# Value tiles of both mixers computed channel by channel and turned on TensorE

## The chip, the cores and the metric

The kernel runs on one core of one Trainium2 chip. The metric is the device time of one execution in microseconds. Four engines matter here: TensorE (PE in the profile) multiplies matrices and transposes, VectorE (DVE) and ScalarE (ACT) work elementwise, GpSimd (POOL) takes some splits of weights and some DMA issues; the SP queue issues the loads of weights.

## The reference, cut to what matters

Four layers over 512 tokens of width 1024: two of a first kind, then two of a second. Each has a mixer and one (first kind) or two (second kind) feed-forward blocks. A mixer begins with one projection `h @ w_in` whose columns are split among its heads:

```python
# first kind
(a_q, a_k, a_v, a_z, a_b, a_a, b_q, b_k, b_v, b_qi, b_ki, b_wi,
 c_q, c_f, c_i, c_g) = jnp.split(h @ w_in[l], SPLIT_POINTS, axis=-1)
vc = to_chunks(i.astype(f32), HG_HEADS, HG_DHEAD)      # c_i: 256 columns
# second kind
sb_q, sb_k, sb_v, fx_q, fx_k, fx_v                      # 256 columns each
```

`c_i` is the value of the gated recurrence HGRN2, `sb_v` and `fx_v` are the values of two attentions. All of them are needed with tokens on the partitions, because the products with them sum over tokens. Everything is float32.

## The kernel before, in words

Activations lie transposed: channels on the 128 partitions, the 512 tokens along the row. A float32 product is made of three: activation and weight are each split into a rounded high part and a low rest (`hh`, `hl`; `wh`, `wl`), and `product` (L1255) issues high by high, high by low and low by high, on L1257, L1258 and L1259.

A **tile** of the projection is 128 columns of `w_in`. `tile` (L1286) keeps a 128x128 block of weights in the array and moves all 512 tokens past it: 8 blocks of the contraction by 3 products, 24 matmuls of 512 columns, into one of PSUM banks 0 to 3. The result has channels on the partitions. `token_tile` (L1295) holds a block of 128 tokens in the array instead and moves the 128 weight columns past it: 4 token blocks by 8 by 3, 96 matmuls of 128 columns. Its result has tokens on the partitions. It is used for the value tiles: the last 2 of the 30 tiles of a first mixer (L1579), the last 4 of the 20 tiles of a second mixer (L1874). Over two layers of each kind that is 4 and 8 tiles, 12 in all.

Each engine runs its own instruction list in order; semaphores join them. For a tile n, SP loads the weights, ACT rounds them to `wh` (`split`, L759) once tile n-2 is done, DVE subtracts to get `wl` (L1991; in a first mixer POOL does the last ten, L691), PE multiplies (`mm_done` counts), and DVE or ACT takes the result out of its bank (`mm_free` counts).

**Around the value tiles of a first mixer.** ACT keeps the last ordinary tile (L960), splits the last weights and then computes gates: four small functions and a square root of the norms of queries and keys (L977 to L983), each behind a load of a function table, and a last table load for the softmax (L841). DVE has been picking the indexer's top keys (`pick`, L2327 to L2330); it waits for `silu_done` 13, which ACT gives after the last ordinary tile, then copies value tile 1 to `hgi` (L2364), makes the last picks, copies value tile 2, and gives `small_copied`. PE waits for that (L1584) and starts the sparse attention: `logits` (L1371), `turned` (L1381), `weighted` (L1393), 16 items in a pipeline over PE, DVE (`top`, `scale`, L2100 to L2107) and ACT (`exp` L841, `copy` L850). Beside it DVE takes the reciprocal of the norms (L2015, at item 0), and PE spreads them over the partitions (L1597, bank 4, every other item); it waits for the reciprocal at item 1.

**Around the value tiles of a second mixer.** DVE's list for tiles 16 to 20 holds splits two tiles ahead, four `fx_norm` of two instructions each (L2734), the copy of tile 16 to `gT` and then four copies of value tiles to `vtok` (L2769). ACT's holds the splits, four square roots, four GELUs on `gT` (L1137) and a table load (L1139). PE then waits until all four banks are free (L1883) and computes `scores(0)` (L1889), the first logits of the stick-breaking attention; ACT makes a softplus of them in three passes (L1145, L1149, L1154), DVE follows (L2790, L2795) with steps of the linear recurrence between (L2709 to L2720), and `scores(1)` waits for the fourth L2790.

Of the kernel before, what the change touches and what calls it, by code (L numbers as in the profile page):

```python
# [12 lines left out]
P = 128  # L13
# [135 lines left out]
def program(nc, a, out):  # L149
    ctx = ExitStack()  # L150
    with ctx:
# [3 lines left out]
        def ev(name):  # L155
            return Event(nc, ctx, name)
# [62 lines left out]
        def take(*shape):  # L219
# [6 lines left out]
            if len(shape) == 1:  # L226
# [153 lines left out]
        y_ready = ev("y_ready")  # L380
        x_ready = ev("x_ready")
        small_done = ev("small_done")
        small_copied = ev("small_copied")
        conv_done = ev("conv_done")
        conv_tap = ev("conv_tap")
        silu_done = ev("silu_done")
# [86 lines left out]
        small2_copied = ev("small2_copied")  # L473
        small_loaded = ev("small_loaded")

        in_mixers = [bc_done, bc_used, ix_go, s_raw, s_turn, small_hi, small_lo, small_done, small_copied,
                     conv_done, conv_tap, silu_done, ix_done, ix_relu, ix_used, lg_done, lg_max, at_exp,
                     at_norm, at_turn, at_copied, at_pv, at_out, g_in, g_abs, g_soft, g_cum, g_turn, g_cols,
                     g_ecol, dn_q, dn_p, dn_v, dn_exp, dn_r, rc_ws, rc_u, rc_o, rc_ds, rc_s, rc_oc, hg_ke,
# [250 lines left out]
        def _(s):  # L730
# [15 lines left out]
            def split(i=None, whole=False, first=None, after_out=False):  # L746
# [14 lines left out]
                place[1] += 1 if half or whole else 0  # L761
                place[2] = 0 if half or whole else 1

            def parts(shift=None):

                for k in range(KD):
                    h_sum.next(s)
                    if shift is None:
                        s.activation(hh[:, k, :], sq[:, k % 4, :], ACT.Copy).then_inc(h_hi.sem, 1)
                    else:  # L770
                        s.activation(hh[:, k, :], sq[:, k % 4, :], ACT.Identity, bias=shift(k))\
                            .then_inc(h_hi.sem, 1)
# [146 lines left out]
            for l in range(DEPTH):  # L919
# [43 lines left out]
                for j in range(22):  # L963
# [8 lines left out]
                    if 8 <= j < 16:  # L972
                        square(dnT[:, j - 8, :])
                s.drain().then_inc(silu_done.sem, 1)

                g_in.next(s)
                link(s.activation(head[:, 3:4], head[:, 0:1], ACT.Exp))  # L977
# [5 lines left out]
                s.activation(std[0:32, 0:P], ps[0:32, 7, 0:P], ACT.Sqrt, bias=epsc[0:32, 0:1])\  # L983
                    .then_inc(std_done.sem, 1)
                n_norm[0] += 1

                softmax(lg, pr, mx, sm, pT)

# [88 lines left out]
            for l in range(DEPTH):  # L1077
# [37 lines left out]

                for n in range(3, 21):
                    split()
                    if n == 4:
                        ff_in.next(s)
                        link(s.activation(ftmp[0:4, :], fF[0:4, :], ACT.Abs))  # L1120
                        link(s.activation(ftmp[0:4, :], ftmp[0:4, :], ACT.Exp, scale=-1.0))
                        s.activation(ftmp[0:4, :], ftmp[0:4, :], ACT.Ln, bias=1.0).then_inc(ff_ln.sem, 1)
                    if 8 <= n < 12:
                        gate(n - 8)
                    if 11 <= n < 15:
                        fx_raw.next(s)
                        square(fxraw[:, n - 11, :])
                    if n == 16:
                        row_root(7, P, 32, 64)
                    if n == 17:  # L1130
                        for j in range(4):
                            lr_rec.next(s)
                            s.activation(lr_t[j], lr_t[j], ACT.Sqrt).then_inc(lr_root.sem, 1)
                    if n == 18:
                        for j in range(4):
                            conv_done.next(s)
                            s.activation(gT[:, j, :], gT[:, j, :], ACT.Gelu_apprx_tanh).then_inc(g_gelu.sem, 1)  # L1137

                s.preload_act_table_set("natural_log_exp_and_others")  # L1139

# [25 lines left out]
                for h in range(4):  # L1166
                    if h < 3:
                        soft(h + 1)
                    for b in range(NT):
                        sb_min.next(s)  # L1170
                        w_ = wsb[:, b, 0:T - b * P]
                        s.activation(w_, w_, ACT.Exp).then_inc(sb_exp.sem, 1)
                lr_y.next(s)
                for j in range(4):
                    square(uT[:, j, :])

# [42 lines left out]
        def _(pe):  # L1219
# [72 lines left out]
                                k == 0, k == KD - 1)  # L1292
                m.then_inc(mm_done.sem, 1)

            def token_tile(N, pool=False):  # L1295

                w, b = parts_ready(pool), bank()
                for n in range(NT):
                    for k in range(KD):
                        m = product(ps[:, b, N * n:N * n + N], hh[:, k, n * P:(n + 1) * P], wh[:, w, k, 0:N],  # L1300
                                    hl[:, k, n * P:(n + 1) * P], wl[:, w, k, 0:N], k == 0, k == KD - 1)
                m.then_inc(mm_done.sem, 1)

            def out_pair(src):

# [233 lines left out]
            for l in range(DEPTH):  # L1539
# [36 lines left out]
                            pe.wait_ge(ix_relu.sem, 12)  # L1576
                        stair_part(n - 9, 8)
                n_norm[0] += 1
                token_tile(P, True)  # L1579
                token_tile(P, True)  # L1580
                place[1] += 16


                small_copied.next(pe)  # L1584
                pe.wait_ge(ix_relu.sem, 12)

                def beside(i):

                    m = i // 2
                    if i % 2 and m < 8:  # L1590
                        if m == 0:
                            pe.wait_ge(rec_done.sem, n_norm[0])
                        else:
                            pe.wait_ge(bc_used.sem, m)
                        for t in range(NT):
                            j = NT * m + t
                            x = pe.matmul(ps[:, BESIDE, t * P:(t + 1) * P], ident[:, j:j + 1].broadcast_to([P, P]),  # L1597
                                          rstd[:, 0:P], start=True, stop=True)
                        x.then_inc(bc_done.sem, 1)
                    if i == 17:  # L1600
                        g_cum.next(pe)
                        pe.wait_ge(bc_used.sem, 8)
                        for n in range(NT):
                            for o, src in enumerate((gg, bet)):
                                at_ = 8 * n + 4 * o
                                x = pe.matmul(ps[:, BESIDE, at_:at_ + 4], src[0:4, n * P:(n + 1) * P],
                                              ident[0:4, 0:4], start=True, stop=True)
                        x.then_inc(g_turn.sem, 1)
# [205 lines left out]
            for l in range(DEPTH):  # L1814
# [41 lines left out]
                for n in range(2, 17):  # L1856
# [12 lines left out]
                    if n == 15:  # L1869
                        small2_copied.next(pe)  # L1870
                        pe.wait_ge(lr_sig.sem, 4)
                        for m in range(4):
                            column_cast(m)
                for n in range(4):  # L1874
                    token_tile(P)
                place[1] += 10

                def scores(h):
# [39 lines left out]
                              start=b == 0, stop=b == NT - 1).then_inc(sb_pv.sem, 1)  # L1918

                scores(0)  # L1920
                for m in range(NT * 4 + 2):
                    if m % NT == 0 and m // NT < 3:
                        scores(m // NT + 1)
                    if m < NT * 4:
                        past(m)
                    if m >= 2:
                        breaks(m - 2)
                pe.wait_ge(nr_used.sem, 4)
                row_sums(4, 4)

                def beside(i):
# [30 lines left out]
        def _(v):  # L1962
# [302 lines left out]
            for l in range(DEPTH):  # L2265
# [93 lines left out]
                mm_done.seen[id(v)][1] += 10  # L2359
                n_mm[0] += 10  # L2360
                v.wait_ge(silu_done.sem, 13)
                for j in range(2):
                    b = filled()
                    v.tensor_copy(hgi[:, :, j * P:(j + 1) * P], ps[:, b, :].rearrange("p (n c) -> p n c", n=NT))  # L2364
                    free()
                    if j:
                        v.sem_inc(small_copied.sem, 1)
                    pick(4)

                def beside(i):  # L2370

# [2 lines left out]
                    if i == 1:  # L2374
                        g_soft.next(v)
                        link(v.tensor_scalar(head[:, 3:4], head[:, 3:4], -1.0, None, ALU.mult))
                        link(v.scalar_tensor_tensor(gg[0:4, :], gg[0:4, :], 0.0, gtmp[0:4, :], ALU.max, ALU.add))
                    if i == 3:
                        link(v.tensor_scalar(gg[0:4, :], gg[0:4, :], head[:, 3:4], None, ALU.mult))
                    if i == 5:  # L2380
                        v.tensor_tensor_scan(gg[0:4, :], reset[0:4, :], gg[0:4, :], 0.0, ALU.mult, ALU.add)\
# [245 lines left out]
            for l in range(DEPTH):  # L2627
# [110 lines left out]
                for n in range(1, 21):  # L2738
# [11 lines left out]
                    if n == 17:  # L2750
                        fx_norm(2)
                        fx_norm(3)
                        v.drain()
                    b = filled()
                    if n <= 2:
                        v.tensor_scalar(sbq[:, n - 1, :], ps[:, b, :], 0.125, None, ALU.mult)
                    elif n <= 4:
                        v.tensor_copy(sbk[0:64, 2 * (n - 3), :], ps[0:64, b, :])
                        v.tensor_copy(sbk[64:128, 2 * (n - 3) + 1, :], ps[64:128, b, :])
                    elif n <= 8:  # L2760
                        j = n - 5
                        taps(uT[:, j, :], b, lambda s_: par[:, 1, B2_CW + 4 * s_ + j:B2_CW + 4 * s_ + j + 1], 4,
                             par[:, 1, B2_CB + j:B2_CB + j + 1])
                    elif n <= 12:
                        v.tensor_copy(fxraw[:, n - 9, :], ps[:, b, :])
                    elif n <= 16:
                        v.tensor_copy(gT[:, n - 13, :], ps[:, b, :])
                    else:
                        v.tensor_copy(vtok[:, :, (n - 17) * P:(n - 16) * P],  # L2769
                                      ps[:, b, :].rearrange("p (n c) -> p n c", n=NT))  # L2770
                    free()
                    if n == 4:
                        ff_ln.next(v)
# [42 lines left out]
                for b in range(5):  # L2816
                    if b < 4:
                        raw(0, b)
                    if b:
                        masked(0, b - 1)  # L2820
                    lr_step(1)
                v.wait_ge(small_loaded.sem, l * 208 + 208)
                for h in range(4):
# [100 lines left out]
```

## Time and profile before

| | |
|---|---|
| Median of three executions | 4055.58 us |
| Lowest and highest | 4048.1 and 4056.75 us |
| The profiled execution's own time | 4050.49 us |
| Its span in the trace | 4048.7 us |
| Mean granted clock of TensorE | 0.97 |
| PE busy | 3819.4 us, 94% |
| DVE busy | 2191.7 us, 54% |
| ACT busy | 1163.6 us, 29% |

The span is what the trace covers; 1.8 us lie around it. Busy shares are averages over stages. In rows of the timeline the first number is the start in us from the span's beginning, the second the length in us, then engine, line, operation, output and input, and in brackets the engine's idle time before it and what ended that.

### The profile page before, as it was taken

Reading aid. Unit: us, or ns where it says so; the run is one execution under the profiler, and the core shown is the slowest. Engines: PE = TensorE matmul, PEld = TensorE weight load, DVE = VectorE, ACT = ScalarE, POOL = GpSimd, SP = SyncE. Lnnn points to the kernel's source line nnn. Section 1 sums busy time; section 2 is a strip of 40 time slices with the busy share of each in tenths; the row PEclk is TensorE's granted clock in tenths of the full one; section 3 lists DMA queues with packets and bytes.
Section 4 is the critical chain, followed back from the end, with each engine's and each line's share of the span. In section 5 each row is a group of like instructions: output and inputs, shape, how many; then the busy total and the mean of one; then the engine's idle time right before and its main releaser. Section 6 shows DMA issues by size and latency. Waiting matters only on the chain.

```text
span 4048.7 us, 50706 instructions
## 1 busy us (share of the span) xinstructions
PE 3819.4 (94%) x18550; PEld 3027.4 (75%) x18550; DVE 2191.7 (54%) x3552; ACT 1163.6 (29%) x1715; POOL 302.2 (7%) x503
## 2 busy tenths in 40 slices
PE   7998889998998889998999998899999999999999
PEld 5778648886777648887888785588878887756887
DVE  4767548854767548855554456355343336444432
ACT  2331323322431323322222234222222223332221
POOL 1110001100020001110110100011000001000000
PEclk9998899999999899999999999999999999999999
DMA  3310025542220025542554320255433332103332
GB/s 87 84 36 1 1 74 161 163 122 78 73 56 1 1 58 162 163 136 82 165 163 122 95 63 1 76 165 164 121 93 94 88 101 74 42 21 83 93 94 94
DMA packets 580037, 359.75 MB, mean 89 GB/s; under 512 B 20398, under 2 KB 559776, under 8 KB 579872
## 3 DMA queue, kind: packets, MB, share of 16 engines
q1 hardware_dynamic: 554464, 281.43, 25.0%
q0 software_dynamic: 25408, 76.11, 6.3%
q8 instruction: 105, 1.72, 0.2%
q14 instruction: 60, 0.49, 0.0%
HBM read 355.35 MB, written 2.10 MB: 88 GB/s over the span
## 4 chain that ended last, share of the span: by engine, by line
PE 87%; DVE 8%; ACT 2%; issue 2%; DVEq 1%; SPq 0%; POOL 0%; DMA 0%; ACTq 0%; POOLq 0%
PE ps L1257 17%; PE ps L1258 17%; PE ps L1259 17%; PE ps L1497 6%; PE ps L1501 6%; PE ps L1500 6%; PE ps L1310 5%; PE ps L1628 3%; PE ps L1413 1%; PE ps L1393 1%; PE ps L1371 1%; PE ps L1790 1%; DVE wl L1991 1%; PE ps L1460 1%; PE ps L1346 1%
## 5 line engine op out<-in xcount | busy, mean ns | idle before, releaser
L1257 PE MATMUL ps<-hh,wh 128*128 128x512 f32 x2816 | 1119.1, 397 | 42.4 <-DVE hl L2050 17.2
L1258 PE MATMUL ps<-hl,wh 128*128 128x512 f32 x2816 | 1103.9, 392 | 0.0
L1259 PE MATMUL ps<-hh,wl 128*128 128x512 f32 x2816 | 1103.7, 392 | 0.0
L1991 DVE TENSOR_TENSOR wl<-wring,wh 128x1024 fp32r<-128x1024 f32 x476 | 581.2, 1222 | 788.9 <-ACT wh L759 782.0
L759 ACT ACTIVATE wh<-wring 128x1024 fp32r<-128x1024 f32 x496 | 522.9, 1056 | 992.5 <-PE ps L1497 506.2
L1257 PEld LDWEIGHTS ps<-hh,wh 128*128 128x128 f32 x2816 | 533.5, 189 | 176.7 <-issue 44.3
L1259 PEld LDWEIGHTS ps<-hh,wl 128*128 128x128 f32 x2816 | 533.0, 189 | 113.0
L1258 PEld LDWEIGHTS ps<-hl,wh 128*128 128x128 f32 x2816 | 534.0, 190 | 108.6 <-issue 1.9
L1497 PE MATMUL ps<-ah,wh 128*128 128x512 f32 x1056 | 411.9, 390 | 2.0 <-DVE wl L1991 2.0
L1501 PE MATMUL ps<-ah,wl 128*128 128x512 f32 x1056 | 410.9, 389 | 0.0
L1500 PE MATMUL ps<-al,wh 128*128 128x512 f32 x1056 | 410.8, 389 | 0.0
L684 POOL DMA_DIRECT2D wada<-in_w_ada x384 | 206.4, 538 | 2059.0 <-DVE ada_sum L2135 1293.7
L1497 PEld LDWEIGHTS ps<-ah,wh 128*128 128x128 f32 x1056 | 198.2, 188 | 43.6 <-DVE wl L1991 2.8
L1501 PEld LDWEIGHTS ps<-ah,wl 128*128 128x128 f32 x1056 | 198.2, 188 | 41.2
L1500 PEld LDWEIGHTS ps<-al,wh 128*128 128x128 f32 x1056 | 198.2, 188 | 40.8
L2139 DVE SCALAR_TENSOR_TENSOR ada_sum<-wada,cact,ada_sum 128x384 f32<-128x384 f32 x288 | 177.8, 617 | 76.1 <-DMA wada<-in_w_ada 34.6
L1310 PE MATMUL ps<-arena,wring 128*128 128x512 f32 x448 | 197.1, 598 | 6.2 <-issue 3.1
L1310 PEld LDWEIGHTS ps<-arena,wring 128*128 128x128 f32 x448 | 84.5, 191 | 117.4 <-issue 114.0
L878 ACT ACTIVATE sq<-ps 128x512 f32<-128x512 f32 x88 | 52.7, 599 | 405.9 <-PE ps L1259 374.7
L1628 PEld LDWEIGHTS ps<-arena 128*128 128x128 f32 x1152 | 135.6, 197 | 20.0 <-ACT arena L994 7.6
L1628 PE MATMUL ps<-arena 128*128 128x128 f32 x1152 | 137.6, 281 | 10.9 <-ACT arena L994 5.4
L2193 DVE TENSOR_TENSOR sq<-sq,ps 128x512 f32<-128x512 f32 x88 | 60.5, 687 | 147.7 <-PE ps L1259 147.7
(396 smaller groups left out, 4041.3 us busy)
## 6 DMA issues: line engine op xcount, KB each, us to landing
wring<-in_w_ffn_up SPq DMA_DIRECT2D x176, 512.0 KB, 4.9
wada<-in_w_ada POOLq DMA_DIRECT2D x384, 192.0 KB, 2.7
wring<-in_w_in SPq DMA_DIRECT2D x98, 512.0 KB, 5.1
wring<-in_ffn_w_up SPq DMA_DIRECT2D x88, 512.0 KB, 5.0
wring<-in_w_ffn_down SPq DMA_DIRECT2D x64, 512.0 KB, 3.6
wring<-in_w_out SPq DMA_DIRECT2D x32, 512.0 KB, 4.9
wring<-in_ffn_w_down SPq DMA_DIRECT2D x32, 512.0 KB, 3.6
wring<-in_w_ffn_down SPq DMA_DIRECT2D x16, 384.0 KB, 3.2
```

Of the source, the lines that this page charges most:

```text
L684: g.dma_start(wada[:, i % 2, :], src[:, m, bass.ds(col + at_, ADA_W)])\
L759: s.activation(wh[:, n_split[0] % 2, :, :], wring[:, p, half, :, :], ACT.Copy).then_inc(w_hi.sem, 1)
L1257: pe.matmul(dst, w, h, start=first, stop=False)
L1258: pe.matmul(dst, w, hlo, start=False, stop=False)
L1259: return pe.matmul(dst, wlo, h, start=False, stop=last)
L1310: m = pe.matmul(ps[:, b, :], wring[:, p, half, k, :], src[:, k, :], start=k == 0, stop=k == KD - 1)
L1497: first = pe.matmul(ps[:, b, :], wh[:, w, j, :], ah[:, at_], start=k == 0, stop=False)
L1500: pe.matmul(ps[:, b, :], wh[:, w, j, :], al[:, at_], start=False, stop=False)
L1501: m = pe.matmul(ps[:, b, :], wl[:, w, j, :], ah[:, at_], start=False, stop=k == NF - 1)
L1628: m = pe.matmul(ps[:, b, n * P:(n + 1) * P], lhsT(n), rhs(n), start=True, stop=True)
L1991: v.tensor_tensor(wl[:, w, :, :], wring[:, p, h, :, :], wh[:, w, :, :].bitcast(F32), ALU.subtract)\
L2139: i = v.scalar_tensor_tensor((ada_out if k == KD - 1 else ada_sum)[:, :], wada[:, k % 2, :], cact[:, k:k + 1], ada_sum[:, :], ALU.mult, AL ...
```

## The change

The 12 value tiles are computed by `tile`, with channels on the partitions. ACT copies each result from its bank to an SBUF buffer and frees the bank (`raw`); PE turns the buffer by four 128x128 transposes into another bank (`turn_raw`); DVE copies that bank to `hgi` or `vtok`, with the shape it had before (`turned`). Three semaphores, `v_raw`, `v_turn` and `v_copied`, take the place of `small_copied`. In a first mixer the buffers are `cbuf`, the turned banks are 4 and 2, and the second tile is turned inside the attention. In a second mixer the buffers are `sq`, the bank is 4, and the fourth tile is turned behind `scores(0)`.

```diff
 # ACT
+            def raw(dst, b, tiles_behind):
+                at_ = mm_done.seen[id(s)]
+                s.wait_ge(mm_done.sem, at_[0] + at_[1] - tiles_behind)
+                s.activation(dst, ps[:, b, :], ACT.Copy).then_inc(v_raw.sem, 1)
+                s.drain().then_inc(mm_free.sem, 1)
...
                 s.drain().then_inc(silu_done.sem, 1)
+                raw(cbuf[:, 0, :], 2, 1)
                 g_in.next(s)
...
                     .then_inc(std_done.sem, 1)
                 n_norm[0] += 1
+                raw(cbuf[:, 1, :], 3, 0)
                 softmax(lg, pr, mx, sm, pT)
...
                 for n in range(3, 21):
                     split()
+                    if n >= 19:
+                        raw(sq[:, n - 19, :], n - 19, 2)
...
+                for j in (2, 3):
+                    raw(sq[:, j, :], j, 3 - j)
                 s.preload_act_table_set("natural_log_exp_and_others")
...
                 lr_y.next(s)
+                s.wait_ge(v_copied.sem, 4)
 # PE
-            def token_tile(N, pool=False):
...
+            def turn_raw(b, src):
+                v_raw.next(pe)
                 for n in range(NT):
+                    m = pe.transpose(ps[:, b, n * P:(n + 1) * P], src[:, n * P:(n + 1) * P], ident[:])
+                m.then_inc(v_turn.sem, 1)
...
-                token_tile(P, True)
-                token_tile(P, True)
+                tile(True)
+                tile(True)
                 place[1] += 16
-                small_copied.next(pe)
-                pe.wait_ge(ix_relu.sem, 12)
+                turn_raw(BESIDE, cbuf[:, 0, :])
+                pe.wait_ge(mm_free.sem, mm_free.seen[id(pe)][0] + mm_free.seen[id(pe)][1] + 2)
...
                     if i % 2 and m < 8:
                         if m == 0:
+                            pe.wait_ge(v_copied.sem, 1)
                             pe.wait_ge(rec_done.sem, n_norm[0])
...
+                    if i == 2:
+                        turn_raw(2, cbuf[:, 1, :])
+                    if i == 4:
+                        pe.wait_ge(v_copied.sem, 2)
...
-                for n in range(4):
-                    token_tile(P)
+                for j in range(4):
+                    tile()
+                    if j == 1:
+                        pe.wait_ge(nr_used.sem, 1)
+                    if j > 1:
+                        pe.wait_ge(v_copied.sem, j - 1)
+                    if j:
+                        turn_raw(4, sq[:, j - 1, :])
...
                 scores(0)
+                pe.wait_ge(v_copied.sem, 3)
+                turn_raw(4, sq[:, 3, :])
 # DVE
                 v.wait_ge(silu_done.sem, 13)
-                for j in range(2):
-                    b = filled()
-                    v.tensor_copy(hgi[:, :, j * P:(j + 1) * P], ps[:, b, :].rearrange("p (n c) -> p n c", n=NT))
-                    free()
-                    if j:
-                        v.sem_inc(small_copied.sem, 1)
-                    pick(4)
+                def turned(b, dst):
+                    v_turn.next(v)
+                    v.tensor_copy(dst, ps[:, b, :].rearrange("p (n c) -> p n c", n=NT)).then_inc(v_copied.sem, 1)
+                pick(4)
+                pick(4)
+                turned(BESIDE, hgi[:, :, 0:P])
...
                     if i == 3:
+                        turned(2, hgi[:, :, P:2 * P])
...
+                    if n > 16:
+                        mm_done.seen[id(v)][1] += 1
+                        n_mm[0] += 1
+                        if n > 17:
+                            turned(4, vtok[:, :, (n - 18) * P:(n - 17) * P])
+                        continue
...
                     if b:
                         masked(0, b - 1)
+                    if b == 2:
+                        turned(4, vtok[:, :, 3 * P:4 * P])
                     lr_step(1)
```

## Rows read from the trace of the kernel before

**Rows 1.** The page, parts 1 and 4: busy time of PE, and the chain by engine

```profile
PE 3819.4 (94%) x18550; PEld 3027.4 (75%) x18550; DVE 2191.7 (54%) x3552; ACT 1163.6 (29%) x1715; POOL 302.2 (7%) x503
...
PE 87%; DVE 8%; ACT 2%; issue 2%; DVEq 1%; SPq 0%; POOL 0%; DMA 0%; ACTq 0%; POOLq 0%
```

**Rows 2.** Timeline of ACT around the value tiles, first mixer of layer 0

```profile
217.00 0.60 ACT L960 ACTIVATE arena<-ps 128x512 f32<-128x512 f32 x1 [3.95 <-PE ps L1259]
...
222.38 0.60 ACT L960 ACTIVATE arena<-ps 128x512 f32<-128x512 f32 x1 [3.84 <-PE ps L1259]
...
224.02 1.28 ACT L977 ACT_TABLE_LOAD   x1
...
232.04 0.36 ACT L983 ACTIVATE std<-ps,epsc 32x128 f32<-32x128 f32 x1
232.42 1.28 ACT L841 ACT_TABLE_LOAD   x1
245.58 0.40 ACT L841 ACTIVATE arena<-arena 128x128 f32<-128x128 f32 x1 [11.88 <-DVE arena L2100]
```

**Rows 3.** Timeline of DVE, the same stretch

```profile
233.15 0.69 DVE L2364 COPY arena<-ps 128x512 f32<-128x512 f32 x1 [14.81 <-PE ps L1259]
233.96 0.69 DVE L2327 MAX8 arena<-arena 128x8 f32<-128x512 f32 x1
...
238.52 0.43 DVE L2330 TENSOR_SCALAR arena<-arena 128x512 f32<-128x512 f32 x1
243.84 0.69 DVE L2364 COPY arena<-ps 128x512 f32<-128x512 f32 x1 [4.90 <-PE ps L1259]
...
245.47 0.94 DVE L2015 RECIPROCAL rstd<-std 32x128 f32<-32x128 f32 x1
...
254.44 0.42 DVE L2100 CUSTOM_DVE_ANT_0 arena<-ps,arena 128x256 f32<-128x256 f32 x1 [3.05 <-issue]
```

**Rows 4.** Timeline of PE, head of that attention

```profile
246.46 2.07 PE L1597 MATMUL ps<-rstd,ident 128*128 128x128 f32 x8 [1.02 <-DVE rstd L2015]
...
248.75 0.42 PE L1381 MATMUL ps<-ident,arena 128*128 128x128 f32 x1
248.96 0.63 PE L1371 MATMUL ps<-arena 128*128 128x128 f32 x2
249.86 0.47 PE L1381 MATMUL ps<-ident,arena 128*128 128x128 f32 x1 [0.26 <-DVE arena L2107]
```

**Rows 5.** Timeline of PE, eight transposes at full clock, earlier in layer 0

```profile
77.35 1.03 PE L1551 MATMUL ps<-ident,arena 128*128 128x128 f32 x8
```

**Rows 6.** Stretches: us, then PE, PEld, DVE, ACT, POOL busy (count), clock, DMA

```profile
233.00:244.00 11.00, 10.73 (x97) 10.59 (x95) 5.62 (x12) 0.70 (x1) 0.00 (x0) 1.00 0.00 0
244.00:262.00 18.00, 15.53 (x61) 11.52 (x62) 11.50 (x42) 4.97 (x20) 0.00 (x0) 0.62 0.00 1
262.00:300.00 38.00, 37.21 (x232) 27.05 (x231) 25.23 (x79) 13.70 (x35) 0.00 (x0) 1.00 0.01 1
```

**Rows 7.** Timeline of ACT around the value tiles, second mixer of its layer 0

```profile
2388.12 1.06 ACT L759 ACTIVATE wh<-wring 128x1024 fp32r<-128x1024 f32 x1 [4.69 <-PE ps L1259]
...
2398.85 1.06 ACT L759 ACTIVATE wh<-wring 128x1024 fp32r<-128x1024 f32 x1 [3.71 <-PE ps L1259]
...
2432.89 1.14 ACT L1145 ACTIVATE arena<-ps 128x512 f32<-128x512 f32 x2 [21.02 <-PE ps L1889]
```

**Rows 8.** Timeline of DVE, the same stretch

```profile
2393.65 0.69 DVE L2767 COPY arena<-ps 128x512 f32<-128x512 f32 x1
...
2401.08 3.04 DVE L2734 SCALAR_TENSOR_TENSOR arena<-arena,lb,ps 64x512 f32<-64x512 f32 x4
...
2420.23 0.69 DVE L2769 COPY arena<-ps 128x512 f32<-128x512 f32 x1 [7.58 <-PE ps L1259]
2430.95 0.69 DVE L2769 COPY arena<-ps 128x512 f32<-128x512 f32 x1 [10.03 <-PE ps L1259]
2435.77 0.69 DVE L2790 SCALAR_TENSOR_TENSOR hT<-ps,arena 128x512 f32<-128x512 f32 x1 [4.13 <-ACT arena L1154]
...
2439.36 0.29 DVE L2790 SCALAR_TENSOR_TENSOR hT<-ps,arena 128x128 f32<-128x128 f32 x1
```

**Rows 9.** Timeline of PE, the first two score groups of that mixer

```profile
2431.72 2.42 PE L1889 MATMUL ps<-arena 128*128 128x512 f32 x8 [0.81 <-DVEq L2090]
2439.70 4.37 PE L1889 MATMUL ps<-arena 128*128 128x512 f32 x8 [5.56 <-DVE hT L2790]
```

More of the change, by code:

```diff
@@ L382, in program @@
         small_done = ev("small_done")
-        small_copied = ev("small_copied")
+        v_raw = ev("v_raw")
+        v_turn = ev("v_turn")
+        v_copied = ev("v_copied")
         conv_done = ev("conv_done")
@@ L474, in program @@
         small_loaded = ev("small_loaded")
-        in_mixers = [bc_done, bc_used, ix_go, s_raw, s_turn, small_hi, small_lo, small_done, small_copied,
+        in_mixers = [bc_done, bc_used, ix_go, s_raw, s_turn, small_hi, small_lo, small_done, v_raw, v_turn, v_copied,
                      conv_done, conv_tap, silu_done, ix_done, ix_relu, ix_used, lg_done, lg_max, at_exp,
@@ L1293, in tile @@
                 m.then_inc(mm_done.sem, 1)
-            def token_tile(N, pool=False):
-                w, b = parts_ready(pool), bank()
+            def turn_raw(b, src):
+                v_raw.next(pe)
                 for n in range(NT):
[L1299 to L1302, printed above, removed]
+                    m = pe.transpose(ps[:, b, n * P:(n + 1) * P], src[:, n * P:(n + 1) * P], ident[:])
+                m.then_inc(v_turn.sem, 1)
             def out_pair(src):
@@ L1928, in _ @@
                 pe.wait_ge(nr_used.sem, 4)
+                pe.wait_ge(v_copied.sem, 4)
                 row_sums(4, 4)
@@ L2358, in _ @@
                 half[0] = 1 - half[0]
-                mm_done.seen[id(v)][1] += 10
-                n_mm[0] += 10
+                mm_done.seen[id(v)][1] += 12
+                n_mm[0] += 12
                 v.wait_ge(silu_done.sem, 13)
-                for j in range(2):
-                    b = filled()
-                    v.tensor_copy(hgi[:, :, j * P:(j + 1) * P], ps[:, b, :].rearrange("p (n c) -> p n c", n=NT))
-                    free()
-                    if j:
-                        v.sem_inc(small_copied.sem, 1)
-                    pick(4)
+                def turned(b, dst):
[4 more added lines that the diff above has]
+                turned(BESIDE, hgi[:, :, 0:P])
                 def beside(i):
@@ L2765, in _ @@
                         v.tensor_copy(fxraw[:, n - 9, :], ps[:, b, :])
-                    elif n <= 16:
+                    else:
                         v.tensor_copy(gT[:, n - 13, :], ps[:, b, :])
-                    else:
-                        v.tensor_copy(vtok[:, :, (n - 17) * P:(n - 16) * P],
-                                      ps[:, b, :].rearrange("p (n c) -> p n c", n=NT))
                     free()
```

## The prediction

> **What bounds the kernel now.** I read the page first: PE is busy 94% of the span and makes up 87% of the chain of work that ended last [rows 1]. Work taken from PE counts unless something else is ready to end the same stretch, so the question for each of the 12 value tiles is which engine is late next. For that I read the timelines of ACT, DVE and PE around the value tiles, first mixer [rows 2 to 4] and second mixer [rows 7 to 9], and then the granted clock [rows 6]. In both places the reader should see the same thing: ACT and DVE sit waiting for PE's last matmul of a tile (11.88 us before ACT's first exponential, 10.03 us before DVE's last copy, 21.02 us before ACT's softplus) [rows 2, 8, 7], while PE has no gap: 97 matmuls fill 10.73 of 11 us at full clock [rows 6]. PE sets the end of the value stretch in all four mixers.
>
> **The price of a tile.** An ordinary tile: ACT takes two of them out at 217.00 and 222.38, both times straight after PE, 5.4 us apart [rows 2]; that is 24 matmuls, 0.224 us each. A value tile: DVE's copies at 233.15 and 243.84 are 10.7 us apart [rows 3], those at 2420.23 and 2430.95 the same [rows 8]; 96 matmuls, 0.111 us each. So a value tile made as an ordinary one takes 5.3 us less of PE, 63.6 us over 12. The rest of the working is what does not reach the end.
>
> What stands against this is a rule for the spacing alone. A matmul of 128 columns costs here half of one of 512, not a quarter. The Trainium skill ("TensorE: Matmul & The Clock Gate", back-to-back issue gap) gives for an isolated bf16 matmul at the high clock columns / 2.4 + 2.5 ns; by that both forms would take about 5.3 us, and the change would gain 2 us before its costs. The same section says that streams with a weight load for each matmul go slower than this at 128 columns. The trace disagrees with the formula and agrees with the caveat: both forms were timed here in the place where they are used, and I go by the rows.
>
> **First mixer, two tiles, one layer.** PE ends tile 2 not at about 243.7 but 2 x 5.3 = 10.6 us earlier, at 233.1. Then step by step:
> - POOL's split takes about as long as for the ordinary tiles before, which ran without a gap, so its weights are in time: 0.
> - ACT now waits for value tile 1 in front of its gate work. The tile ends at 222.3 + 5.4 = 227.7; the copy takes 0.60 as at 222.38 [rows 2], a drain 0.1, so the gate work begins at 228.5 in place of 224.02: 4.5 us later. The root of the norms, at 232.04 before, ends at 232.40 + 4.5 = 236.9 [rows 2]. Queued behind the wait are all the gate functions, that root and the table load for the softmax.
> - DVE has the picks (4.99 us, from 233.96 to 238.95 [rows 3]) to do between 224 and 229, hidden under the two tiles. The first turned copy is hidden too (0.69, at about 233.8).
> - The attention's head needs the reciprocal of the norms, because PE spreads it at item 1 before it goes on [rows 4]. Before, that reciprocal began at 245.47 [rows 3], held back by DVE's second copy. Now it can begin at 236.95, held back by ACT. **Gain 8.5 us, not 10.6**: what is late next is ACT's gate work.
> - The second raw copy (0.6) and the table load (1.28) stand between root and first exponential, which comes at 238.8, 1.9 us behind the start of the reciprocal in place of 0.1. PE turned the first item 3.3 us behind that start (248.75 [rows 4] less 245.47 [rows 3]) and needs the exponential plus about 1.0 us of DVE, 2.9 us: it just fits, 0 to 0.3 lost.
> - PE turns value tile 2 at item 2, at half clock (the clock averaged 0.62 from 244 to 262 [rows 6]). Two logit matmuls and a transpose start 0.21 us apart there (248.75 to 248.96 [rows 4]), so four transposes cost 0.85; at full clock eight end 1.03 us after the first begins, some 0.45 for four [rows 5]. PE waited 0.26 for DVE just behind [rows 4]. I take 0.85, between 0.2 and 1.1.
> - DVE's second turned copy (0.69) falls at item 3, ahead of 3.05 us in which DVE did nothing [rows 3]: 0. PE's wait for it at item 4 comes later than that: 0.
>
> Net 8.5 - 0.9 = 7.6 us; for two layers **15.2 us**.
>
> **Second mixer, four tiles, one layer.** PE begins value tile 1 at 2388.0, where ACT's split was waiting for the tile before [rows 7]. The order of the splits has to keep up with 5.4 us a tile:
> - ACT splits tile 18's weights at 2388.12, has its GELUs until about 2395.1 (the last waits for DVE's copy at 2393.65 [rows 8]), and splits tile 19's at 2395.1 where it waited until 2398.85 before [rows 7]. DVE follows at 2396.2 and is done at 2397.4; PE wants the weights at 2398.9. Margin 1.5 us.
> - DVE's norm step, 3.04 us [rows 8], then runs to 2400.5, its split for tile 20 to 2401.8; PE wants that at about 2404.8. Margin 3 us. All raw and turned copies (0.6 and 0.69) fit in the idle time of both engines.
> - PE turns tiles 1 and 2 between products, 0.45 us each at full clock [rows 5], 0.9 in all. Tile 3's turn lies beside ACT's copy of tile 4, which frees the last bank as DVE's copy of 0.69 did before [rows 8]: 0. ACT loads its table behind that copy now (1.28, as in rows 2) while PE starts the scores, 1.2 us ahead of the first softplus pass (2431.72 [rows 9] to 2432.89 [rows 7]): 0 to 0.3.
> - DVE's fourth turned copy falls among the four L2790, which run back to back with the recurrence from 2435.77 to 2439.36 [rows 8]; PE's second scores wait for the last of them [rows 9]. 0.6 to 0.7 on the path.
>
> Net 4 x 5.3 - 0.9 - 0.65 - 0.15 = 19.5 us; for two layers **39.0 us**.
>
> Sum: 15.2 + 39.0 = 54.2 us off the profiled execution's own 4050.5 us, 3996.3. Its median of three is 4055.6, 5 us above, and the lowest 4048.1; I allow 2 us for that and forecast **3998 us**, 1.4% less. A measurement of this kernel tells about 0.2%, 8 us, from no change.
>
> **What is not in the rows.** How PE's clock behaves when it idles at a new moment. Before, it fell at the head of the first attention: a mean of 0.62 over 18 us with PE busy 15.5 us [rows 6], so some 13.7 us at half clock. Had all been at full clock, up to 6 us less; another such stretch, up to 6 us more. PE will idle again at this head, now from 233.6 to 238 and wholly, so I take the same low stretch, and 3 us either way for the pair of layers.
>
> **Rivals.**
> - **A: PE's whole gain arrives.** The gate work on ACT is short enough, or the attention does not wait for the reciprocal: 10.6 - 0.9 in a first mixer, in all 58 us, 3992 to 3994. For: ACT was idle 11.88 us [rows 2]. Against: of these, 4.5 + 1.9 are used up and the reciprocal is needed at item 1 [rows 4]. 12%.
> - **B: the handovers cost more.** Each of 12 turns waits for ACT and DVE across semaphores, or the split order stalls tile 3 of a second mixer (margin 1.5 us): 1 us more per tile, 12 us, 4010. For: ACT is now in front of PE in each tile. Against: the margins above. 12%.
> - **C: slower, by the clock.** After its wait at the attention's head PE stays at half clock. From 262 to 300 PE is busy 37.2 of 38 us at clock 1.00 [rows 6]; at half of it that would take up to 37 us longer. It decides from 54 / 4, some 14 us per mixer, which is 14 us of full-clock work done at half clock; all of that stretch low in four mixers gives +94 us, 4145. For: a wholly idle PE of 4 us is new. Against: the clock came back after 13.7 us in the trace under just such mixed work [rows 6]. 2%.
> - **D: a tile costs the same in either form**, so nothing is gained and 12 turns and waits remain: 12 x 0.3 to 0.8, 4054 to 4060. This is the formula of the skill quoted above; against it stand two timings in rows 2, 3 and 8. 2%.
>
> The forecast itself has 72%, with a range of its own of 3990 to 4006. A and B carry the range to **3986 to 4010**. Faster by over 0.2%: forecast, A, B, 96%; within: 2%; slower: 2%.
>
> **What would show it.** Right: 512-column groups on L1257 to L1259 with 12 x 24 matmuls more and no 128-column ones left; the new ACT copies following PE's last matmul; in the first mixer PE idle about 4 us ahead of L1597 with the reciprocal behind ACT's root, the root 4.5 us behind its old distance from the last kept tile; the second mixer's first scores 43.7 - 20.2 = 23.5 us behind the split that was at 2388.12. Wrong: matmuls of a value tile more than 0.23 us apart, an idle PE between value tiles of a second mixer, a clock of 0.5 beyond the first 20 us of an attention, or first scores later than 25 us.

## The result, and the profile after

The change made the kernel faster: ratio 0.9854 of the times before, 95% interval 0.9827 to 0.988. The median of four executions is 3994.3 us (3986.5 to 4005.0) against 4056.2 us (4048.1 to 4057.1). The forecast was 3998 us in a range of 3986 to 4010. The profiled execution took 4004.99 us by itself, its span 4003.3 us: it is the slowest of the four, and only 45.5 us shorter than the profiled one before, where 54.2 were forecast. The medians differ by 61.9 us. Where the other 9 of the profiled execution went is a question for the experiments.

The page of the changed kernel, part 1 (PE), part 4 (the chain by engine) and part 5 (one of the three product lines):

```profile
PE 3773.6 (94%) x17734; PEld 2970.2 (74%) x17734; DVE 2190.5 (55%) x3552; ACT 1169.6 (29%) x1727; POOL 302.3 (8%) x503
...
PE 86%; DVE 8%; ACT 3%; issue 2%; DVEq 1%; SPq 0%; ACTq 0%; POOL 0%; DMA 0%; POOLq 0%
...
L1273 PE MATMUL ps<-hh,wh 128*128 128x512 f32 x2912 | 1158.0, 398 | 42.2 <-DVE hl L2078 16.9
```

L1273 to L1275 are L1257 to L1259 of before. Each has 2912 matmuls of 512 columns in place of 2816: 96 more, 3 x 96 = 12 tiles x 24. PE has 816 instructions less: 12 x (96 - 24) = 864 less for the products, 48 more for the transposes. The chain is what it was but for a percent that passed from PE to ACT [rows 1].

**First mixer of layer 0.** Timeline of ACT, answering to [rows 2]:

```profile
222.55 0.60 ACT L969 ACTIVATE arena<-ps 128x512 f32<-128x512 f32 x1 [3.83 <-PE ps L1275]
...
227.99 0.60 ACT L770 ACTIVATE arena<-ps 128x512 f32<-128x512 f32 x1 [3.89 <-PE ps L1275]
228.69 1.28 ACT L987 ACT_TABLE_LOAD   x1
...
236.71 0.36 ACT L993 ACTIVATE std<-ps,epsc 32x128 f32<-32x128 f32 x1
236.97 0.57 ACT L770 ACTIVATE arena<-ps 128x512 f32<-128x512 f32 x1
237.64 1.28 ACT L850 ACT_TABLE_LOAD   x1
238.93 0.40 ACT L850 ACTIVATE arena<-arena 128x128 f32<-128x128 f32 x1
```

Timeline of DVE, the same stretch, answering to [rows 3]:

```profile
233.94 0.69 DVE L2393 COPY arena<-ps 128x512 f32<-128x512 f32 x1 [4.72 <-PE ps L1315]
...
237.10 0.94 DVE L2043 RECIPROCAL rstd<-std 32x128 f32<-32x128 f32 x1 [2.26 <-ACT std L993]
...
242.56 0.68 DVE L2393 COPY arena<-ps 128x512 f32<-128x512 f32 x1
...
244.43 0.42 DVE L2128 CUSTOM_DVE_ANT_0 arena<-ps,arena 128x256 f32<-128x256 f32 x1 [0.81 <-DVE arena L2409]
```

Timeline of PE, answering to [rows 4, 5] (L1315 are the new transposes):

```profile
233.23 0.60 PE L1315 MATMUL ps<-ident,arena 128*128 128x128 f32 x4
233.67 0.61 PE L1385 MATMUL ps<-arena 128*128 128x128 f32 x4
238.19 1.47 PE L1612 MATMUL ps<-rstd,ident 128*128 128x128 f32 x8 [3.91 <-DVE rstd L2043]
...
240.27 1.06 PE L1315 MATMUL ps<-ident,arena 128*128 128x128 f32 x4
241.13 0.63 PE L1385 MATMUL ps<-arena 128*128 128x128 f32 x2
```

Stretches of the changed kernel, columns as in [rows 6]:

```profile
222.00:233.20 11.20, 11.20 (x51) 9.23 (x50) 4.77 (x10) 6.56 (x9) 3.70 (x3) 1.00 0.44 129
...
238.20:256.00 17.80, 16.83 (x90) 12.07 (x91) 13.77 (x51) 8.02 (x29) 0.00 (x0) 0.90 0.01 1
```

What to see: the reciprocal that the attention's head needs now waits 2.26 us for ACT's root (it had waited for DVE's copies before), and PE idles 3.91 us ahead of L1612. Measured from the last kept tile, the reciprocal begins 14.55 us later (222.55 to 237.10), before 23.09 (222.38 to 245.47): 8.54 us won. The four transposes at full clock cost 0.44 us (233.23 to 233.67), those inside the attention at half clock 0.86 (240.27 to 241.13). One thing is not as forecast: the stretch at the attention's head had a mean clock of 0.90, not 0.62 [rows 6].

**Second mixer of its layer 0.** Timeline of ACT, answering to [rows 7]:

```profile
2381.72 1.06 ACT L761 ACTIVATE wh<-wring 128x1024 fp32r<-128x1024 f32 x1 [4.69 <-PE ps L1275]
...
2388.64 1.04 ACT L761 ACTIVATE wh<-wring 128x1024 fp32r<-128x1024 f32 x1
...
2392.60 1.06 ACT L761 ACTIVATE wh<-wring 128x1024 fp32r<-128x1024 f32 x1 [2.43 <-PE ps L1275]
...
2404.45 0.60 ACT L770 ACTIVATE sq<-ps 128x512 f32<-128x512 f32 x1 [5.32 <-PE ps L1275]
2405.14 1.28 ACT L1154 ACT_TABLE_LOAD   x1
2406.44 0.99 ACT L1160 ACTIVATE arena<-ps 128x512 f32<-128x512 f32 x2
```

Timelines of DVE and PE there, answering to [rows 8] and [rows 9]:

```profile
2404.89 0.69 DVE L2393 COPY arena<-ps 128x512 f32<-128x512 f32 x1 [5.22 <-PE ps L1315]
2409.18 0.69 DVE L2823 SCALAR_TENSOR_TENSOR hT<-ps,arena 128x512 f32<-128x512 f32 x1 [3.61 <-ACT arena L1169]
...
2412.32 0.68 DVE L2393 COPY arena<-ps 128x512 f32<-128x512 f32 x1
...
2413.37 0.29 DVE L2823 SCALAR_TENSOR_TENSOR hT<-ps,arena 128x128 f32<-128x128 f32 x1
```

```profile
2404.25 0.60 PE L1315 MATMUL ps<-ident,sq 128*128 128x128 f32 x4
2405.13 2.42 PE L1914 MATMUL ps<-arena 128*128 128x512 f32 x8 [0.28 <-ACTq L771]
```

From the split for tile 18 to the first scores it took 2405.13 - 2381.72 = 23.41 us. The prediction has 23.5 there, from 43.7; the rows give 43.6 (2388.12 to 2431.72), so its own figure should have been 23.4. To the first softplus pass it took 24.72 us (2406.44 - 2381.72) in place of 44.77, 20.05 less. DVE's turned copy at 2412.32 stands between the softplus steps: they take 4.19 us from first to fourth, before 3.59 (2435.77 to 2439.36).

### The profile page after: what moved, and what is told of

Read it like the earlier page. It is cut to its first block, busy times and chain, and to the rows that moved or that the text cites. A ratio compares the mean times of both kernels' runs of the same rounds, so it can differ in the third digit from the quotient of the medians.

```text
span 4003.3 us, 49102 instructions
## 1 busy us (share of the span) xinstructions
PE 3773.6 (94%) x17734; PEld 2970.2 (74%) x17734; DVE 2190.5 (55%) x3552; ACT 1169.6 (29%) x1727; POOL 302.3 (8%) x503
## 4 chain that ended last, share of the span: by engine, by line
PE 86%; DVE 8%; ACT 3%; issue 2%; DVEq 1%; SPq 0%; ACTq 0%; POOL 0%; DMA 0%; POOLq 0%
PE ps L1273 17%; PE ps L1274 16%; PE ps L1275 16%; PE ps L1511 6%; PE ps L1515 6%; PE ps L1514 6%; PE ps L1324 5%; PE ps L1647 3%; PE ps L1427 1%; PE ps L1407 1%; PE ps L1809 1%; PE ps L1385 1%; DVE wl L2019 1%; PE ps L1474 1%; PE ps L1360 1%
## 5 line engine op out<-in xcount | busy, mean ns | idle before, releaser
L1273 PE MATMUL ps<-hh,wh 128*128 128x512 f32 x2912 | 1158.0, 398 | 42.2 <-DVE hl L2078 16.9
L1274 PE MATMUL ps<-hl,wh 128*128 128x512 f32 x2912 | 1142.3, 392 | 0.0
L1275 PE MATMUL ps<-hh,wl 128*128 128x512 f32 x2912 | 1141.6, 392 | 0.0
L1273 PEld LDWEIGHTS ps<-hh,wh 128*128 128x128 f32 x2912 | 551.9, 190 | 179.9 <-issue 43.9
L1275 PEld LDWEIGHTS ps<-hh,wl 128*128 128x128 f32 x2912 | 551.8, 189 | 117.2
L1274 PEld LDWEIGHTS ps<-hl,wh 128*128 128x128 f32 x2912 | 552.6, 190 | 112.7 <-issue 1.9
L1511 PEld LDWEIGHTS ps<-ah,wh 128*128 128x128 f32 x1056 | 198.2, 188 | 43.6 <-DVE wl L2019 2.8
L1647 PE MATMUL ps<-arena 128*128 128x128 f32 x1152 | 138.4, 282 | 10.4 <-ACT arena L1005 4.9
```

The source lines that it names most:

```text
L1273: pe.matmul(dst, w, h, start=first, stop=False)
L1274: pe.matmul(dst, w, hlo, start=False, stop=False)
L1275: return pe.matmul(dst, wlo, h, start=False, stop=last)
L1511: first = pe.matmul(ps[:, b, :], wh[:, w, j, :], ah[:, at_], start=k == 0, stop=False)
L1647: m = pe.matmul(ps[:, b, n * P:(n + 1) * P], lhsT(n), rhs(n), start=True, stop=True)
```

## The experiments

Ratios are to the kernel before, which ran on the same chip beside each group.

**The changed kernel once more**, for a second profile.

> The changed kernel once more, for a second profile. Theory 1 (place by place): the value tiles and their heads give what they gave in the first profile in every execution (7 to 11 us in a first mixer by the attention, 20 us in a second mixer by the first softplus pass), and the 9.5 us that the first profile lost after that, from 7.9 us ahead at the start of layer 0's delta recurrence to 1.6 us behind at its end, are half-clock time that fell there in that execution; in a second profile that loss is absent or elsewhere. Rival 2 (the change slows the recurrence): it is there again, 8 us or more. Ratio by theory 1 0.984 to 0.988, 3990 to 4000 us.

Measured: ratio 0.9857 (0.9835 to 0.9879), median 3994.6 us. The heads gave what they gave. But layer 0's recurrence was slow again: its first output came 7.5 us ahead of before (386.98 against 394.45), its eighth 2.2 us behind (426.17 against 423.97). In the first profile it was 7.7 us ahead at the first output and 1.8 behind at the root of the norms that follows the eighth (430.58 against 428.81). ACT's outputs of the recurrence (one per chunk of 64 tokens) in the kernel before:

```profile
394.45 0.38 ACT L1029 ACTIVATE hT<-ps 128x256 f32<-128x256 f32 x1 [6.66 <-PE ps L1708]
400.51 0.38 ACT L1029 ACTIVATE hT<-ps 128x256 f32<-128x256 f32 x1 [5.68 <-PE ps L1708]
404.49 0.38 ACT L1029 ACTIVATE hT<-ps 128x256 f32<-128x256 f32 x1 [3.60 <-PE ps L1708]
```

and in the changed kernel's first profile:

```profile
386.71 0.38 ACT L1040 ACTIVATE hT<-ps 128x256 f32<-128x256 f32 x1 [6.66 <-PE ps L1727]
393.93 0.38 ACT L1040 ACTIVATE hT<-ps 128x256 f32<-128x256 f32 x1 [6.83 <-PE ps L1727]
401.14 0.38 ACT L1040 ACTIVATE hT<-ps 128x256 f32<-128x256 f32 x1 [6.83 <-PE ps L1727]
407.35 0.38 ACT L1040 ACTIVATE hT<-ps 128x256 f32<-128x256 f32 x1 [5.83 <-PE ps L1727]
411.33 0.38 ACT L1040 ACTIVATE hT<-ps 128x256 f32<-128x256 f32 x1 [3.60 <-PE ps L1727]
```

And two stretches of the changed kernel that lie in it (columns as in [rows 6]):

```profile
386.00:401.00 15.00, 15.00 (x68) 14.02 (x67) 4.10 (x12) 0.77 (x2) 0.00 (x0) 0.50 0.00 0
401.00:430.60 29.60, 27.59 (x185) 23.72 (x184) 13.31 (x34) 5.79 (x12) 0.00 (x0) 0.80 0.01 1
```

A chunk takes 7.21 us at half clock (the first stretch) and 3.98 at full clock; for that, a stretch of the kernel before:

```profile
404.60:429.00 24.40, 22.13 (x184) 19.92 (x182) 12.76 (x34) 5.86 (x12) 0.00 (x0) 1.00 0.01 2
```

Before, one step was slow (6.06 us), now three are (7.22, 7.21 and 6.21). PE is busy all the time in the slow stretch, so this is not a wait.

**One mixer kind alone.** The change in the second mixers, then in the first mixers, the other kind as before (`token_tile` and `small_copied` kept for it).

> The change in the second mixers alone, the first mixers as before. Prediction's sum: 19.5 us per layer, 39.0 us, ratio 0.990. If the handovers cost 1 us more per tile (rival B): 31 us, 0.992. In its profile the gap between the split for tile 18 and the first softplus pass should be 23.3 to 23.6 us in place of 44.8.

> The change in the first mixers alone. Prediction's sum: 7.6 us per layer, 15.2 us, ratio 0.996. If the changed kernel's first profile is the rule and the recurrence gives it back (rival 2): about 6 us in all, 0.9985. If the shorter half-clock stretch at the attention's head is a lasting part of the gain (11 us per layer): 22 us, 0.9945.

Measured: second alone 0.9905 (0.9888 to 0.9922), median 4010.8 us, 38.5 us less; first alone 0.9963 (0.9947 to 0.9979), median 4035.2 us, 15.0 us less than 4049.65. The sums of the prediction were 39.0 and 15.2. The figure of 23.3 to 23.6 us in the first of these expectations names the wrong end: it holds for the first scores, the softplus pass is 1.3 us behind (24.72 in the changed kernel, and 24.72 here: 2387.23 to 2411.95). Rival B (31 us) lies just outside the interval (0.9922 is 31.6 us), and so does a lasting gain of 22 us in the first mixers (0.9947 is 21.5 us); the 6 us of rival 2 lie outside it too (0.9979 is 8.5 us).

**The form of the tile alone**: only what PE multiplies is changed; the turn is left out.

```diff
-                token_tile(P, True)
-                token_tile(P, True)
+                tile(True)
+                tile(True)
...
-                    token_tile(P)
+                    tile()
```

> The 12 value tiles are made with channels on the partitions, and DVE copies them as before; the turn into token order, ACT's copy and the second bank are left out, so the values enter the attentions and the recurrence in the wrong order. This is the price of the tile's form alone: 5.3 us for each of 12 tiles; in a first mixer 0.8 us less of it arrives, because DVE's last picks (4.99 us) then end between the two copies at 233.7 in place of 233.2. Sum 62 us, ratio 0.9847. The changed kernel against it shows what the handover costs: by the prediction 8 us (54 against 62). If both forms cost the same (rival D): 1.000.

Measured: 0.9831 (0.9812 to 0.985), median 3984.0 us; that is 68 us (61 to 76), where 62 were expected. Rival D is out: the two forms do not cost the same. Against the changed kernel of the same group (3994.6) it is 10.7 us faster, where 8 were expected. Rows of it, ACT and then DVE (before's line numbers):

```profile
2365.96 1.06 ACT L759 ACTIVATE wh<-wring 128x1024 fp32r<-128x1024 f32 x1 [4.69 <-PE ps L1259]
...
2389.66 1.14 ACT L1145 ACTIVATE arena<-ps 128x512 f32<-128x512 f32 x2 [10.45 <-PE ps L1889]
```

```profile
234.21 0.94 DVE L2015 RECIPROCAL rstd<-std 32x128 f32<-32x128 f32 x1
```

Split to softplus takes 23.70 us here and 24.72 with the turns: 1.0 us for the handovers of a second mixer as far as this pass, where the prediction had 0.9 + 0.15. In a first mixer its last kept tile was at 221.22, so the reciprocal begins 12.99 us behind, against 14.55 with the turns.

**ACT's first raw copy moved behind the gate work**, and **with it DVE's fourth turned copy** moved behind the softplus steps (both moves).

```diff
                 s.drain().then_inc(silu_done.sem, 1)
-                raw(cbuf[:, 0, :], 2, 1)
...
                 n_norm[0] += 1
+                raw(cbuf[:, 0, :], 2, 1)
                 raw(cbuf[:, 1, :], 3, 0)
...
-                    if b == 2:
+                    if b == 4:
                         turned(4, vtok[:, :, 3 * P:4 * P])
```

> The changed kernel, with ACT's copy of a first mixer's value tile 1 moved behind the gate work and the root of the norms. The root then ends at 232.4 again in place of 236.9, both raw copies follow it, and what is late next is DVE's first turned copy (about 234.0 to 234.6): the reciprocal begins at 234.9 in place of 237.1. Theory 1 (ACT's gate work behind the new wait set the head): 2.2 us less at the reciprocal and 3 to 4 at the first exponential, per layer, 4 to 7 us in all, ratio 0.9843 to 0.985. Rival (the head is set by PE's turn and DVE): no change, 0.986. The clock's low stretches will again fall elsewhere, several us either way in one execution.

> The same, and in a second mixer DVE's turned copy of value tile 4 moved from among the four softplus steps (after the third) to after the fourth. By theory 1 it then lies in the 3.3 us in which DVE waits for the next softplus: 0.6 us less per layer for the second scores, 1.2 in all; ratio 0.984 to 0.985. If the copy was hidden anyway: as gates_first.

Measured: first move alone 0.9843 (0.9825 to 0.9862), median 3993.5 us; both 0.983 (0.9815 to 0.9846), median 3980.8 us. DVE of the first move alone (its last kept tile at 221.35):

```profile
232.75 0.69 DVE L2392 COPY arena<-ps 128x512 f32<-128x512 f32 x1 [4.72 <-PE ps L1314]
...
233.56 0.94 DVE L2042 RECIPROCAL rstd<-std 32x128 f32<-32x128 f32 x1
```

The reciprocal begins 12.21 us behind the kept tile, 2.34 less than in the changed kernel (14.55), and right behind DVE's turned copy. ACT's first exponential comes 12.88 us behind the kept tile (234.23), in the changed kernel 16.38 (238.93 - 222.55): 3.50 us less, where 3 to 4 were expected. So ACT's gate work behind the new wait was what held the head, and DVE is next, as expected. DVE of both moves, in a second mixer:

```profile
2384.15 0.69 DVE L2822 SCALAR_TENSOR_TENSOR hT<-ps,arena 128x512 f32<-128x512 f32 x1 [3.61 <-ACT arena L1168]
...
2387.74 0.29 DVE L2822 SCALAR_TENSOR_TENSOR hT<-ps,arena 128x128 f32<-128x128 f32 x1
...
2389.61 0.68 DVE L2392 COPY arena<-ps 128x512 f32<-128x512 f32 x1
```

First to fourth step take 3.59 us again: 0.60 won per layer as far as this step.

**Dead work ahead of layer 0's recurrence**, in the changed kernel:

```diff
                 dn_q.next(pe)
+                for _ in range(80 if l == 0 else 0):
+                    pe.transpose(ps[:, 0, 0:P], ident[:], ident[:])
```

> The changed kernel with 80 dead transposes (8.7 us at full clock) on PE ahead of layer 0's gated delta rule, so that this stage and the recurrence start where they started in the kernel before (delta recurrence's first output near 394.4 in place of 386.7). Theory 1b (the loss in layer 0's recurrence comes from when the stage starts relative to the clock's changes, not from the change's own work): the low stretch in the recurrence is 13.7 us again in place of 27.3 and 34.1, the recurrence takes 9 us less, and the dead work is paid back: the end of that recurrence comes within 2 us of where it was. Rival 2 (something in the change slows the recurrence): low stretch still 27 us or more, everything from there 8.7 us later, 4003 us median.

Measured: 0.9885 (0.987 to 0.99), median 4004.8 us, 7.8 to 10.5 us more than the changed kernel's medians (3994.3 to 3997.0), which ran in other groups. Rival 2 had 4003 us. In its profile the recurrence's first outputs are:

```profile
392.46 0.38 ACT L1040 ACTIVATE hT<-ps 128x256 f32<-128x256 f32 x1 [6.65 <-PE ps L1729]
399.68 0.38 ACT L1040 ACTIVATE hT<-ps 128x256 f32<-128x256 f32 x1 [6.83 <-PE ps L1729]
405.89 0.39 ACT L1040 ACTIVATE hT<-ps 128x256 f32<-128x256 f32 x1 [5.83 <-PE ps L1729]
409.88 0.38 ACT L1040 ACTIVATE hT<-ps 128x256 f32<-128x256 f32 x1 [3.60 <-PE ps L1729]
```

Two slow steps (7.22 and 6.21 us), neither one (theory 1b) nor three (rival 2). The recurrence began at 392.46, not near 394.4 as meant, and this execution was already 1.3 us ahead of the changed kernel's first profile at the last kept tile (221.26 against 222.55). Its eighth output came at 425.38, there 422.84, and the root behind it at 430.21, there 430.58. So of the 5.75 us between the first outputs a part was gained back by the end of the recurrence in this execution. Over its executions the dead work was not paid back. Each theory is half right: the length of the low stretch changes with the start of the stage, but no gain in time is shown. At equal clock (last table below) the dead work costs 4.1 us, less than its own 8.7, but four executions in a group without the changed kernel can't settle that.

From the first to the eighth output layer 0's recurrence took, in the profiles, what the third column says. The last two columns split each execution in two: at ACT's split for tile 18 in the first of the second mixers, behind both first mixers, and from there to the end of the span.

| kernel | first output at | first to eighth, us | split for tile 18 at | from there to the end, us |
|---|---|---|---|---|
| before | 394.45 | 29.5 | 2388.12 | 1660.6 |
| second mixers alone | 393.49 | 29.5 | 2387.23 | 1620.1 |
| changed, three profiles | 386.71, 386.98, 385.78 | 36.1, 39.2, 36.1 | 2381.72, 2378.39, 2370.25 | 1621.6, 1621.8, 1621.9 |
| first mixers alone | 386.44 | 36.1 | 2371.07 | 1660.2 |
| form alone | 379.10 | 29.5 | 2365.96 | 1619.2 |
| first move | 382.05 | 36.1 | 2369.82 | 1622.0 |
| both moves, two profiles | 376.57, 383.21 | 29.7, 36.1 | 2356.68, 2371.07 | 1619.9, 1619.7 |
| dead work | 392.46 | 32.9 | 2379.97 | 1621.9 |

The loss of 7 to 10 us is no fixed cost of the change: one profile of both moves, which does the same work, is without it, and so is the form alone, though both start the recurrence earlier still. It is no chance of single executions either: all three profiles of the changed kernel have it, and those of the first mixers alone and of the first move. What it goes by is not shown.

Behind the split, where only the second mixers are changed, the three profiles of the changed kernel gain 39.0, 38.8 and 38.7 us (39.0 forecast). Ahead of it, where only the first mixers are changed, they gain 6.4, 9.7 and 17.9 us (15.2 forecast), and the first mixers alone 17.0. So what the profiles differ by lies ahead of the split. There the rest of layer 0 decides, work that the change does not touch: from the recurrence's eighth output to the last kept tile of layer 1 it takes 727.3 us before (mean clock 0.96), 728.7 in the changed kernel's first profile (0.95), but 719.2 and 718.6 in the other two and 718.3 with the first mixers alone (0.97 each). All three profiles of the changed kernel lose in the recurrence; two get as much or nearly as much back behind it, the first does not, and that is about its missing 9 us.

**The changed kernel and both moves on one chip.**

> The changed kernel on one chip with the next, for their difference. Theory 1: ratio to the kernel before 0.984 to 0.987.

> The version with both moves again. By the heads of its stages (2 to 4 us less in a first mixer, 0.6 in a second) 5 to 9 us less than the changed kernel, ratio 0.982 to 0.985; if the first comparison's 11 us were chance, no difference.

Measured: 0.9851 (0.9821 to 0.9882) and 0.9842 (0.9814 to 0.987), medians 3997.0 and 3996.1 us. The raw times do not tell the two apart: 0.9 us, where the heads had promised 5 to 9. They scatter with the clock, which the results list for each execution: the twelve executions of first mixers alone reach from 4020.75 us at a mean clock of 0.974 to 4049.71 at 0.966. I fitted one slope to 93 executions (one level per kernel), which gives -3.4 us for each 0.001 of mean clock, and read each kernel at 0.970, with what is left as scatter (3.2 us; without the slope 7.7). One execution of the changed kernel is left out: it is listed with a mean clock of 0.926 and took 3993.6 us like its neighbours, where the slope would add some 150 us. With it in, the slope is -0.5 and the changed kernel's level 58.4 us below the one before, so the table rests on leaving it out:

| kernel | executions | at clock 0.970, us | less than before |
|---|---|---|---|
| before | 37 | 4051.8 +- 1.1 | |
| changed | 13 | 3997.2 +- 1.8 | 54.5 |
| second mixers alone | 6 | 4010.3 +- 2.6 | 41.5 |
| first mixers alone | 12 | 4036.7 +- 1.8 | 15.1 |
| form alone, no turn | 5 | 3990.9 +- 2.9 | 60.9 |
| first move | 5 | 3989.4 +- 2.8 | 62.3 |
| both moves | 11 | 3994.2 +- 2.0 | 57.6 |
| dead work | 4 | 4001.3 +- 3.2 | 50.5 |

The +- are 95% bounds of the fit; they leave out differences between chips. Both moves is 3.1 us faster than the change by this reading (0.4 to 5.6 by the fit); the heads of the stages say 5.9 (2 x 2.34 + 2 x 0.60). That the first move alone reads lower than both moves shows how far such a reading can be trusted: some 5 us.

## Why the prediction was right

- **The price of a tile** held: the value stretch of the first mixer is full (PE 11.20 of 11.20 us) and the tiles are 5.4 us apart; 12 tiles less their handovers gave 54.5 us at equal clock, 54.2 were forecast. By raw medians the three groups gave 61.9, 55.0 and 64.0 us. The formula of the Trainium skill ("TensorE: Matmul & The Clock Gate", back-to-back issue gap) for isolated matmuls, weighed against it in the prediction, would have given 2 us before costs; the runs disagree with it.
- **First mixer.** What was late next was named: ACT's gate work. The root ended 4.5 us later against the kept tile, the reciprocal began 8.54 us earlier (8.5 forecast), the first exponential 1.83 us behind it (1.9), the turn at half clock cost 0.86 us (0.85), DVE's second turned copy lay in idle time. The kernel with the change in the first mixers alone gave 15.0 us (15.2). Of the 10.6 us that PE saves in the mixer the prediction left 10.6 - 8.5 = 2.1 us behind; moving ACT's copy alone won 2.34 us, so that was this copy. How the parts add up is in some measure luck, though. In layer 1 the reciprocal came 8.63 us earlier against the kept tile, as in layer 0, but the recurrence's first output 10.4 us earlier in the changed kernel's first profile (1312.46 - 1151.54 = 160.92 in place of 1322.62 - 1151.31 = 171.31), 10.5 and 10.4 in the other two and 11.1 with the first mixers alone, where the prediction has 7.6. That and the clock's gains and losses in layer 0 lie on both sides of 15.2 and about cancel.
- **Second mixer.** First scores 23.41 us behind the split (23.4), the split order without a stall (tile 19's weights split at 2388.64, tile 20's at 2392.60 with 2.43 us of waiting ahead), table load level with the scores, DVE's copy 0.60 us on the path. Alone: 38.5 us (39.0), and 38.7 to 39.0 behind the split in the changed kernel's three profiles. The prediction's 43.7 us should have been 43.6, which makes 23.4 us; no step hangs on it.
- **Rival A** fell with the wait of 2.26 us for the root. Its total did not decide it: the measured median (3994.3) fits its 3992 to 3994 as well as the forecast. **Rival B** fell with 1.0 us of handovers in a second mixer as far as the softplus, not 4. **Rival C**, slower by the clock, did not come: the attention's head was at half clock for a shorter time (0.90 mean, not 0.62). What did stand at half clock for longer was layer 0's recurrence, which no rival named. **Rival D** fell with the form alone.
- **The term that was off** is "I take the same low stretch" at the attention's head. There the clock was better by some 3 us, and the attention was 11.2 us ahead at its seventh item (ACT's exponential started at 248.92 us, before at 260.13) in place of 7.6. The next stages gave it back: 7.7 us ahead at the recurrence's first output, 1.8 behind at the root after it. In the prediction the clock stood as 3 us either way; the profiles of the changed kernel show a loss of 7 to 10 us in this one stage, and two of the three a gain of 8 to 9 behind it. The profiled execution had the loss without the gain, and so 45.5 us where the levels at equal clock differ by 54.5.

## What to carry to other kernels

When a matmul can be written either way round, let the long dimension move past the array and pay for a transpose of the result: here 24 matmuls and 4 transposes replaced 96, for 5.3 us less per tile against about 0.5. Place the extra copies by asking what is queued behind them: the same copy held the reciprocal 2.3 us ahead of ACT's gates and no longer behind them, and held the fourth softplus step 0.6 us when it stood among them and no longer after. Where single executions differ by 10 us or more, compare the distances between two events of one stage, or times at equal granted clock, before blaming the change for what its profile shows elsewhere.

## What the runs showed of the hardware that was not expected

- PE stayed at the half level (1.2 GHz) with PE busy in the profile for 15.00 of 15 us (386 to 401) in the recurrence, and rose to 2.4 GHz in the same kind of work later. The rows don't show what makes it rise: with the start of the stage anywhere from 376.57 to 394.45 us, between one and four steps were slow.
- The time of an execution goes with its mean granted clock, 3.4 us for each 0.001 (scatter 3.2 us about the slope, 7.7 without it), with a spread of 29 us in twelve executions of one kernel. One execution of 94 does not fit: 0.926 with an ordinary time.
- At a granted clock of 1.00, a 128-column matmul with its own weight load starts 0.111 us after the one before, a 512-column one 0.224 to 0.227 us; four times the columns cost twice the time.
